# Attention of a hybrid diffusion trunk: equal pieces of keys for both row halves, and the squares of the difference outputs moved to GpSimd

## The reference, cut to what matters

```python
def gqa_block(q, k, v):
    s = einsum('bqkgd,bskd->bkgqs', q, k) * (HEAD_DIM ** -0.5)
    p = softmax(s, axis=-1)
    return einsum('bkgqs,bskd->bqkgd', p, v)

def diff_block(q, k, v, lam):
    s = einsum('bqhmd,bshmd->bhmqs', q, k) * (HEAD_DIM ** -0.5)
    p = softmax(s, axis=-1)
    p = p[:, :, 0] - lam * p[:, :, 1]
    return einsum('bhqs,bshe->bqhe', p, v)
...
d_out = sweep_query_blocks(lambda qb: diff_block(qb, dk_all, dv_all, lam), dq)
diff_out = rms_norm(d_out, diff_sub_norm[l]) * (1.0 - lam_init)
```

## Time and profile before

| | |
|---|---|
| runs | 2391.0, 2390.71, 2385.99 us (median 2390.71) |
| profiled execution | 2387.86 us, its span 2386.1 us |
| TensorE's granted clock | 0.992 of full speed in the mean |
| busy | PE 2310.7 us (97%), PEld 2139.7 (90%), DVE 1495.4 (63%), ACT 1065.7 (45%), POOL 194.7 (8%) |
| attention, layer 0 | 322.6 to 461.2 us of the span: 138.6 us |
| attention, layer 1 | 1497.6 to 1631.2 us: 133.6 us |

### The profile page before, as it was taken

One profiled execution on the slowest core, in us unless ns is written; L12 is line 12 of the kernel. 1 busy time (PEld: TensorE's weight loads), 2 busy tenths in 40 slices (PEclk: granted clock), 3 DMA queues, 4 the chain that ended last, 5 costly groups with the idle time before them and its releaser, 6 DMA issues. The chain is left out here.

```text
span 2386.1 us, 40526 instructions
## 1 busy us (share of the span) xinstructions
PE 2310.7 (97%) x16311; PEld 2139.7 (90%) x16311; DVE 1495.4 (63%) x2403; ACT 1065.7 (45%) x2121; POOL 194.7 (8%) x160
## 2 busy tenths in 40 slices
PE   7999999899999999999999999999999999999999
PEld 5877877799999999999997777778999999999998
DVE  5335568677664865747643565787676658467473
ACT  5433357644442642524346333674444345344252
POOL 1330000100003000000215200010000110000000
PEclk9999999999999999999999999999999999999999
DMA  9225440122225223232231163102222432323222
GB/s 299 96 68 172 143 152 28 45 80 80 75 94 159 63 79 88 81 98 68 93 125 53 51 199 120 33 1 71 80 80 80 159 81 73 105 62 98 65 73 84
DMA packets 246666, 224.01 MB, mean 94 GB/s; under 512 B 6945, under 2 KB 232305, under 8 KB 245969
## 3 DMA queue, kind: packets, MB, share of 16 engines
q1 hardware_dynamic: 242528, 219.25, 29.7%
q0 software_dynamic: 480, 0.66, 0.3%
q10 hardware_dynamic: 3472, 1.52, 0.2%
HBM read 211.70 MB, written 9.70 MB: 93 GB/s over the span
## 5 line engine op out<-in xcount | busy, mean ns | idle before, releaser
L2352 ACT ACTIVATE ring_high<-raw 128x512 fp32r<-128x512 f32 (+1 forms) x278 | 158.1, 609 | 250.0 <-PE ps L2706 150.4
L2492 DVE TENSOR_TENSOR ring_low<-raw,ring_high 128x512 fp32r<-128x512 f32 (+1 forms) x278 | 204.5, 761 | 69.3 <-ACT ring_high L2352 65.1
L2771 PE MATMUL ps<-hH,ring_low 128*128 128x320 f32 x640 | 197.9, 309 | 0.3
L2771 PE MATMUL ps<-hH,ring_high 128*128 128x320 f32 x640 | 197.8, 309 | 0.0
L2771 PE MATMUL ps<-hL,ring_high 128*128 128x320 f32 x640 | 197.8, 309 | 0.0
L1564 DVE SCALAR_TENSOR_TENSOR xT<-ps,mod,xT 128x512 f32<-128x512 f32 (+1 forms) x128 | 64.0, 545 | 193.4 <-PE ps L2706 193.4
L359 PE MATMUL ps<-wH,hL 128*128 128x512 f32 (+1 forms) x460 | 176.5, 384 | 5.2 <-DVE wL L871 2.6
L359 PE MATMUL ps<-wH,hH 128*128 128x512 f32 (+1 forms) x460 | 171.0, 372 | 0.0
L2706 PE MATMUL ps<-gH,ring_low 128*128 128x320 f32 x704 | 160.9, 310 | 0.3 <-DVE xT L1564 0.3
L2706 PE MATMUL ps<-gL,ring_high 128*128 128x320 f32 x704 | 160.4, 309 | 0.0
L2706 PE MATMUL ps<-gH,ring_high 128*128 128x320 f32 x704 | 160.3, 309 | 0.0
(11 more groups left out here) (384 smaller groups left out, 6194.8 us busy)
## 6 DMA issues: line engine op xcount, KB each, us to landing
raw<-in_w_in SPq DMA_DIRECT2D x56, 1024.0 KB, 5.4
raw<-in_w_ffn_in SPq DMA_DIRECT2D x88, 512.0 KB, 5.2
gmod<-in_w_mod SPq DMA_DIRECT2D x24, 1024.0 KB, 8.6
raw<-in_w_ffn_out SPq DMA_DIRECT2D x16, 1024.0 KB, 5.1
b_raw<-in_w_branch SPq DMA_DIRECT2D x22, 512.0 KB, 4.4
head_w<-in_w_mod SPq DMA_DIRECT2D x8, 1024.0 KB, 12.4
modw<-in_w_mod SPq DMA_DIRECT2D x8, 1024.0 KB, 7.6
raw<-in_w_out SPq DMA_DIRECT2D x8, 1024.0 KB, 5.8
```

The costliest lines, as they stand in the source:

```text
L2352: nc.scalar.activation(ring_block(m.ring_high, b, src.shape[1], src.shape[2]), src, ACT.Copy).then_inc(m.sem("w_high"), 1)
L2492: nc.vector.tensor_tensor(ring_block(m.ring_low, b, nk, cols), src, ring_block(m.ring_high, b, nk, cols).bitcast(F32), ALU.subtract).then_ ...
L2771: last = nc.tensor.matmul(m.ps[:, plan.banks[n, 0][BANK[what]], 0:HALF], w[:, k, :], a[:, k, :], start=(first and k == 0 and q == 0), stop ...
```

## The change

Four things change, all inside `attention`.

1. Scores are laid out so that the keys stand in the same order for both halves: latent tiles 0 and 1, the cached tile, latent tiles 2 and 3. A half now begins 128 columns into the first bank and 640 columns later begins the other, without a gap, so both halves cross a bank's border after the same number of keys. Each half is scored by three matmuls (256, 128 and 256 keys) in place of two: six in place of four. The middle bank now holds the last 256 keys of the low half and the first 256 of the high half, so the wait (`middle_scored`) is of the last matmul, 256 keys of the high half, for the first, 256 keys of the low half.
2. For "diff" one instruction of 640 columns replaces L1492 and L1494.
3. The squares leave ACT. GpSimd computes them into a buffer `o_sq` of 5 x 4 x 128 columns, each just before its product with the gain; it now waits for the output's copy out of PSUM, and the product waits for the square.
4. DVE sums them, one reduction of 4 x 128 columns for each of the five query blocks: four rounds after the block's last difference step, or behind the last round for the two blocks where that is too late.

```diff
-        self.o_sq = at("o_sq", [P, 2, P], a + 26624)
+        self.o_sq = at("o_sq", [P, TT, 4, P], 0)
...
-KEYS = [[0, 1, 2, 3, TT], [TT, 0, 1, 2, 3]]
+KEYS = [0, 1, TT, 2, 3]
...
-        return bass.AP(flat_set.tensor, flat_set.offset, [list(flat_set.ap[0]), [896, 2], [1, T]])
+        return bass.AP(flat_set.tensor, flat_set.offset + P, [list(flat_set.ap[0]), [T, 2], [1, T]])
...
-                    nc.tensor.matmul(m.ps[:, b + 1, 0:P], m.rq[low, qb, pos, :], m.kv[low, kb[0], TT, :],
-                                     start=True, stop=True).then_inc(m.sem("tail_scored"), 1)
...
-                    pe.wait_ge(m.sem("tail_scored"), sum(x[1] < CTX for x in steps[:s + 1]))
-                    last = nc.tensor.matmul(m.ps[:, b + 1, 384:512], m.rq[high, qb, pos, :], m.kv[high, kb[1], TT, :],
-                                            start=True, stop=True)
+                    last_keys, cached, first_keys = slice(2, 4), slice(TT, TT + 1), slice(0, 2)
+
+                    def keys(rows, block, tiles, bank_, at):
...
+                    keys(low, kb[0], last_keys, b + 1, 0).then_inc(m.sem("middle_scored"), 1)
+                    keys(high, kb[1], last_keys, b + 2, P)
+                    keys(low, kb[0], cached, b, 3 * P)
+                    keys(high, kb[1], cached, b + 2, 0)
+                    keys(low, kb[0], first_keys, b, P)
+                    pe.wait_ge(m.sem("middle_scored"), sum(x[1] < CTX for x in steps[:s + 1]))
+                    last = keys(high, kb[1], first_keys, b + 1, 2 * P)
...
         def _(pool):
             for s, (kind, qt, j) in enumerate(steps):
                 if kind in ("diff", "ctx diff"):
+                    pool.wait_ge(*freed(o_chunk[s]))
                     for i in range(1 if kind == "diff" else 2):
+                        o = m.rq[:, 4 + j + i, qt, :]
+                        nc.gpsimd.tensor_tensor(m.o_sq[:, qt, j + i, :], o, o, ALU.mult).then_inc(m.sem("o_squared"), 1)
                         pool.wait_ge(m.sem("o_squared"), squares[s] + i + 1)
-                        o = m.rq[:, 4 + j + i, qt, :]
                         nc.gpsimd.tensor_tensor(o, o, m.subn[:, L, :], ALU.mult).then_inc(m.sem("pool_order"), 1)
...
-                    nc.scalar.activation(m.o_sq[:, n % 2, :], m.rq[:, 4 + j + i, qt, :], ACT.Square,
-                                         accum_out=m.sml[:, g:g + 1]).then_inc(m.sem("o_squared"), 1)
...
-                    nc.vector.scalar_tensor_tensor(out=e[:, 0:512], in0=e[:, main], scalar=a[:, 6:7], in1=e[:, 0:512],
-                                                   op0=ALU.mult, op1=ALU.add)
-                    nc.vector.scalar_tensor_tensor(out=e[:, 512:T], in0=e[:, tail_], scalar=a[:, 6:7], in1=e[:, 512:T],
+                    nc.vector.scalar_tensor_tensor(out=e[:, 0:T], in0=e[:, T:2 * T], scalar=a[:, 6:7], in1=e[:, 0:T],
                                                    op0=ALU.mult, op1=ALU.add).then_inc(m.sem("e_ready"), 1)
...
+            def sum_squares(qt, last):
+                dve.wait_ge(m.sem("o_squared"), squares[last] + (2 if kind_of[last] == "ctx diff" else 1))
+                order.step(nc.vector.tensor_reduce(m.sml[:, 0:4 * TT].rearrange("p (j t) -> p t j", t=TT)[:, qt, :],
+                                                   m.o_sq[:, qt, :, :], AX.X, ALU.add))
```

More of the change, by code:

```diff
@@ L1226, in attention @@
     turn_chunk = {x[6]: c for c, x in enumerate(chunks) if x[6] is not None}
+    last_of = {qt: max(s for s, x in enumerate(steps) if x[1] == qt and x[0] in ("diff", "ctx diff")) for qt in range(TT)}
     squares = [sum({"diff": 1, "ctx diff": 2}.get(k, 0) for k in kind_of[:s]) for s in range(S)]
@@ L1298, in scores @@
                         qb, pos, kb = 4 + j, qt, (j, j)
-                    nc.tensor.matmul(m.ps[:, b + 1, 0:P], m.rq[low, qb, pos, :], m.kv[low, kb[0], TT, :],
-                                     start=True, stop=True).then_inc(m.sem("tail_scored"), 1)
[L1301 to L1304, removed]
-                    pe.wait_ge(m.sem("tail_scored"), sum(x[1] < CTX for x in steps[:s + 1]))
-                    last = nc.tensor.matmul(m.ps[:, b + 1, 384:512], m.rq[high, qb, pos, :], m.kv[high, kb[1], TT, :],
-                                            start=True, stop=True)
+                    last_keys, cached, first_keys = slice(2, 4), slice(TT, TT + 1), slice(0, 2)
+                    def keys(rows, block, tiles, bank_, at):
+                        n = (tiles.stop - tiles.start) * P
+                        return nc.tensor.matmul(m.ps[:, bank_, at:at + n], m.rq[rows, qb, pos, :],
+                                                m.kv[rows, block, tiles, :].rearrange("p t c -> p (t c)"),
+                                                start=True, stop=True)
+                    keys(low, kb[0], last_keys, b + 1, 0).then_inc(m.sem("middle_scored"), 1)
[5 more added lines that the diff above has]
+                    last = keys(high, kb[1], first_keys, b + 1, 2 * P)
                 else:
@@ L1328, in values @@
                         for half in range(2):
-                            last = nc.tensor.matmul(out[half * HD:(half + 1) * HD, 0:P], m.kv[:, 9, KEYS[half][n], v],
+                            last = nc.tensor.matmul(out[half * HD:(half + 1) * HD, 0:P], m.kv[:, 9, KEYS[n], v],
                                                     eT[:, 5 * half + n, :], start=(n == 0), stop=(n == 4))
@@ L1332, in values @@
                     for n in range(5):
-                        last = nc.tensor.matmul(out[:, 0:P], eT[:, n, :], m.kv[:, 4 + j, KEYS[0][n], :],
+                        last = nc.tensor.matmul(out[:, 0:P], eT[:, n, :], m.kv[:, 4 + j, KEYS[n], :],
                                                 start=(n == 0), stop=(n == 4))
@@ L1448, in _ @@
                     copy(i - 1, c)
-                if i >= 3 and kind_of[i - 3] in ("diff", "ctx diff"):
-                    square(i - 3)
                 if i == (35 if more else 28):
                     next_high(nc, m, act, nxt)
-            square(S - 1)
         @block.vector
@@ L1488, in weigh @@
                     dve.wait_ge(*done)
-                    tail_, main = slice(T, T + P), slice(T + P, 2 * T)
-                    nc.vector.scalar_tensor_tensor(out=e[:, 0:512], in0=e[:, main], scalar=a[:, 6:7], in1=e[:, 0:512],
-                                                   op0=ALU.mult, op1=ALU.add)
-                    nc.vector.scalar_tensor_tensor(out=e[:, 512:T], in0=e[:, tail_], scalar=a[:, 6:7], in1=e[:, 512:T],
+                    nc.vector.scalar_tensor_tensor(out=e[:, 0:T], in0=e[:, T:2 * T], scalar=a[:, 6:7], in1=e[:, 0:T],
                                                    op0=ALU.mult, op1=ALU.add).then_inc(m.sem("e_ready"), 1)
@@ L1549, in _ @@
                         ins.then_inc(m.sem("chunk_copied_dve"), 1)
+                for qt, last in last_of.items():
+                    if i == last + 4:
+                        sum_squares(qt, last)
                 if i == (36 if more else 30):
                     next_low(nc.vector, m, dve, nxt)
+            for qt, last in last_of.items():
+                if last + 4 >= S + 2:
+                    sum_squares(qt, last)
             order.step(affine(nc, m, dve, order, L, 1))
```

## The result

The changed kernel takes 2393.87 us in the median of 13 runs (2391.59 to 2397.31); the kernel before, run beside it, takes 2389.97 (13 runs, 2384.59 to 2391.83). The ratio is 1.0025, with a 95% interval of 1.0018 to 1.0032: slower by 6.0 us (4.3 to 7.7). The forecast was 2396 us and +6.9. The profiled execution took 2392.59 us (span 2390.8), 4.7 more than the one before.

A forecast was written before the change was run, and what follows sets the result against it. TensorE was taken to set the pace in the middle of both attention stages. Stall 5.9, ScalarE and product -2, stage ends 3.0, clock 0 gave +6.9 us; 2394.8 or 2397.6 by baseline, said as 2396, range 2387 to 2402.

The forecast's parts named there:

- The stall: In each score group, the last matmul's row half stands still 0.11 us behind the wait: +5.9 us, between 0 and 7.0.
- the guess that the groups at the ends count half: Of 64 score groups, the 21 at stage ends lose half to the wait, 1.2 us, as other waits can swallow it.
- The further matmuls: Score groups: four extra passes with loads, hidden beside running streams: 0; bound 0.21 us a group, 13 us in all.
- the term that was mis-sized: ScalarE's removed squares and the single product shorten TensorE's waits for copies at layer ends: -2 us, between 0 and 5 gained.
- The rival of ScalarE as the pace: Each of 32 latent-block squares gives 0.3 us, 9.6 us; -6.6 with the end and no stall: 2381 to 2384; chance 0.1.
- One product: On VectorE, 640 columns take 0.89 us, saving 0.11 us on each of 32 steps, off TensorE's path in the middle.
- GpSimd's port: Forecast: nothing in sum. Rival: squares and products block VectorE until it bounds the kernel, +6.4 us more, 2401 to 2404; chance 0.15.
- The tail: Attention ends: last squares, reduction and small preparations delay the next stage 1.85 and 1.15 us, +3.0; between 1.5 and 4.5.
- The clock behind the stage: After each attention TensorE runs at 1.2 GHz for 3.4 us; change taken as 0, 0.9 us a layer each way.

The follow-up runs named there:

- the layout alone: Kernel before with the new key order, six score matmuls a group and one product, squares still on ScalarE: 1.0022 against before, +5.3 us.
- far producer: Kernel before with equal key order, halves 896 columns apart, five matmuls a group, the awaited one of 128 columns, one product; squares on ScalarE: 0.9998 against before.
- late producer: Changed kernel with the awaited matmul moved behind the low half's cached keys, so it ends 0.21 us later: 1.0083 against before.
- Six matmuls without the stall: Kernel before with both matmuls of 512 columns cut into two of 256, layout and wait as before: 1.0006 against before.
- far producer on top of after: Changed kernel with halves 896 columns apart and five matmuls a group, the awaited one of 128 columns: 1.0005 against before.
- short tail: Changed kernel with both squares of a context step ahead of their products and the small preparations ahead of the last two sums: 1.0029 against before.
- far producer and the short tail: Changed kernel with halves 896 columns apart, an awaited matmul of 128 columns, and context squares before products, small preparations before the last sums: 1.0001 against before.

## Why the prediction was right

**The stall: right, in place and size.** Forecast 0.11 us in a group and 5.9 in all. A group is 0.10 longer and so is each interval; the layout alone costs 5.3 us, and against the equal amounts with a far producer (1.0022 against 0.9998) 5.7, some 3 us each way. By the bodies it is less, 139.66 - 137.25 = 2.4 and 2.2 us, 4.6 in sum, which is 46 groups at 0.10: the guess that the groups at the ends count half was near. The stream of the last score starts 0.76 us behind the group's first, where 0.75 was said, and a pair of steps lasts 0.20 longer (7.01 to 7.21), where 0.22 was said. The forecast had the high half free 0.21 us behind the producer's stream, and 0.16 + 0.05 + 0.11 = 0.32 for the record, the start and the load. The late producer leaves 0 of the 0.21 and lost 0.22 more a group, 0.32 in all, which is that sum.

**The further matmuls: right, nearly 0.** Six matmuls without the stall run in 1.35 us a group and add 0.3 us to the two bodies.

**ScalarE: the term that was mis-sized.** I took -2 us, because TensorE stood 0.82 us for a copy behind a square. The runs show well under 1. In layer 0 the bodies without and with the squares on ScalarE are 136.93 and 136.95 in the old layout, 137.10 and 137.25 with the far producer, 139.43 and 139.66 in the changed layout: 0.0 to 0.2 us. In layer 1, without the delays, they are 130.45 and 130.72, 130.44 and 130.96, 132.64 and 133.14: 0.3 to 0.5. The whole is below what the ratios can show. That the wait at the place of the earlier trace rows gave back so little is a measurement; what else ends near it, so that a square less moves it so little, stays open. The rival of ScalarE as the pace is refuted for the change's direction, and holds in part for the other: 40 more squares cost 9 us.

**One product: right.** 0.885 us where 0.89 was read from a slope, hidden as said; 1.9 us less busy time in 87 moved nothing.

**GpSimd's port: right in effect, wrong in detail.** One L1475 in four is stretched, by up to 0.17 us, and five of the 32 rows of L1487, which was expected to lose nothing, by 0.28. That is 4.3 us in both layers, and VectorE has it to spare. TensorE's intervals are the same with squares on GpSimd (3.38 in the far producer on top of after) as without (3.38). At the stage's end the square beside L328 took 2.38 us where 0.40 is usual, and ended 0.26 us behind it. The Trainium skill's page "SBUF — State Buffer", section "Who interferes with whom", says that a VectorE instruction in a two-port mode, or one with two inputs from SBUF beside a GpSimd instruction that reads SBUF, shares ports with GpSimd: the one that began first holds them for its whole length, and the other is fully blocked. By that an L1475 that starts 0.03 us into a square would lose the other 0.37; it loses 0.17. The square behind L328 agrees within 0.14: blocked to the end, it would have ended 0.40 behind L328.

**The tail: right mechanism, 0.4 too large.** Forecast +1.85 and +1.15, measured +1.60 and +0.97. The reduction was 0.69 as taken; the squares were 0.40 and not 0.45, so the last one ended 1.69 us behind the output in layer 0 and not 1.96. The clock behind the stage, taken at 0, was 0 for this change: TensorE works at half clock for 3.26 us behind layer 0 and 3.40 behind layer 1, against 3.3 and 3.4 before.

**The sum.** By bodies and tails, without the delays, the parts are: stall +4.6, the layout without it +0.5, the squares off ScalarE -0.7, tails +2.6, in sum +7.0. The forecast had +5.9, 0, -2 and +3.0, in sum +6.9. ScalarE's smaller gain and the layout's own price made it 1.8 us too low, the stall and the tails 1.7 too high, so that the sum is nearer than its terms, which is luck in part. The whole kernel measured +6.0.

## What to carry to other kernels

When a wait of TensorE on its own matmul is moved, count the time from the end of the producer's stream to the moment that the waiting matmul's row half is free: here 0.64 us was enough and 0.21 was not, by 0.10 us in each of 64 groups, and most of it reached the end. Equal pieces win nothing while both row halves are busy anyway; the two parts of this change that saved work took it from engines that waited for TensorE. Before relieving an engine for a wait that names it, ask what else ends near that wait: doubling the load there cost 9 us, removing it brought 0.5 us or less a layer.

## What the hardware showed beyond expectation

How much of TensorE's work falls into the stretch at half clock behind an attention varies between kernels whose last microseconds differ. Behind layer 0 it is 3.26 us of work in after, 4.20 with the short tail, and 5.08 with the far producer and the short tail, in this row of its trace:

```profile
462.60:469.40 6.80, 5.08 (x19) 5.11 (x20) 4.18 (x7) 5.03 (x8) 1.36 (x4) 0.50 0.00 0
```

That is up to 0.9 us at stake where the work moved by one or two. And the passes of the two row halves don't start in program order: L1303 starts its first pass at 378.66, L1301, issued ahead of it for the other half, its second at 378.87; so each half has a stream of its own.
